# Mean squares of seven norms: partial sums on VectorE in place of products on TensorE

## The reference

```
def rms_norm(x, gain):
    x32 = x.astype(jnp.float32)
    y = x32 * lax.rsqrt(jnp.mean(x32 * x32, axis=-1, keepdims=True) + RMS_EPS)
    return (y * gain.astype(jnp.float32)).astype(x.dtype)
```

## Time and profile before

| what | value |
|---|---|
| median of 3 runs | 3530.77 us |
| profiled execution, its own time | 3534.64 us |
| its span, first to last instruction | 3532.8 us |
| TensorE matmuls busy | 3387.8 us (96%) |
| VectorE busy | 1567.7 us (44%) |
| ScalarE busy | 1187.9 us (34%) |
| GpSimd busy | 1297.5 us (37%) |
| mean granted TensorE clock | 0.983 of full speed |

### The profile page before, as it was taken

How to read it: one execution, slowest core, us unless ns; L and a number is a source line. 1 busy time by engine, 2 the same in 40 slices (tenths; PEclk the granted TensorE clock), 3 DMA queues, 4 the chain that set the end, 5 groups by cost and what they waited for, 6 DMA issues and landing times.

```text
span 3532.8 us, 41630 instructions
## 1 busy us (share of the span) xinstructions
PE 3387.8 (96%) x15852; PEld 2725.5 (77%) x15852; DVE 1567.7 (44%) x2863; ACT 1187.9 (34%) x1638; POOL 1297.5 (37%) x562
## 2 busy tenths in 40 slices
PE   7979999999999999999999999887999999999998
PEld 4667776887888888888888887575788868878886
DVE  5816115996454431165666662417211124642112
ACT  4425223323333333232222222334322234433221
POOL 3320233443333334444444443234344433434442
PEclk9989999999999999999999999999999999999999
DMA  2230222343555456576666663121233322123332
GB/s 106 75 108 25 78 95 74 107 147 111 187 180 193 165 202 200 161 203 188 185 186 190 190 186 117 60 92 34 90 96 94 92 87 72 42 66 95 96 96 78
DMA packets 424645, 428.08 MB, mean 121 GB/s; under 512 B 146720, under 2 KB 343968, under 8 KB 422704
## 3 DMA queue, kind: packets, MB, share of 16 engines
q1 hardware_dynamic: 424496, 426.00, 38.4%
HBM read 354.63 MB, written 69.21 MB: 120 GB/s over the span
## 4 chain that ended last, share of the span: by engine, by line
PE 69%; issue 13%; DVE 11%; POOL 5%; ACT 1%; DMA 1%; SPq 1%; POOLq 0%; DVEq 0%; PEldq 0%; ACTq 0%
PE pb L632 20%; PE pb L633 20%; PE pb L634 20%; POOL s_over L563 5%; PE pb L894 3%; PE pb L649 1%; PE pb L818 1%; DVE s_sq L1539 1%; DVE s_arena L1760 1%; DVE s_arena L1754 1%; DVE s_hS L1553 1%; DMA s_ring<-w 1%; PE pb L803 1%; SPq L443 1%; DVE s_arena L1719 1%
## 5 line engine op out<-in xcount | busy, mean ns | idle before, releaser
L563 POOL TENSOR_TENSOR s_over<-s_ring,s_rhigh 128x1024 fp32r<-128x1024 f32 x518 | 1252.5, 2419 | 2166.3 <-ACT s_rhigh L1168 2166.0
L1168 ACT ACTIVATE s_rhigh<-s_ring 128x1024 fp32r<-128x1024 f32 x518 | 548.7, 1060 | 1504.5 <-DMA s_ring<-w 677.9
L632 PE MATMUL pb<-s_over,s_rhigh 128*128 128x512 f32 x2112 | 835.8, 396 | 0.0
L634 PE MATMUL pb<-s_over,s_over 128*128 128x512 f32 x2112 | 833.7, 395 | 0.0
L633 PE MATMUL pb<-s_over,s_rhigh 128*128 128x512 f32 x2112 | 833.7, 395 | 0.0
L632 PE MATMUL pb<-s_hS,s_rhigh 128*128 128x512 f32 (+1 forms) x1888 | 763.2, 404 | 44.3 <-DVE s_hS L1553 39.8
L634 PE MATMUL pb<-s_hS,s_over 128*128 128x512 f32 (+1 forms) x1896 | 737.3, 389 | 0.0
L633 PE MATMUL pb<-s_hS,s_rhigh 128*128 128x512 f32 (+1 forms) x1888 | 734.9, 389 | 0.0
L633 PEld LDWEIGHTS pb<-s_over,s_rhigh 128*128 128x128 f32 x2112 | 397.2, 188 | 95.6 <-issue 1.2
L632 PEld LDWEIGHTS pb<-s_over,s_rhigh 128*128 128x128 f32 x2112 | 397.2, 188 | 95.5 <-issue 1.2
L634 PEld LDWEIGHTS pb<-s_over,s_over 128*128 128x128 f32 x2112 | 397.2, 188 | 94.5
(11 more groups left out here) (244 smaller groups left out, 2727.1 us busy)
## 6 DMA issues: line engine op xcount, KB each, us to landing
s_ring<-w SPq DMA_DIRECT2D x272, 512.0 KB, 3.5
s_ring<-eu SPq DMA_DIRECT2D x128, 512.0 KB, 4.0
s_ring<-ev SPq DMA_DIRECT2D x128, 512.0 KB, 4.2
acts<-s_arena SPq DMA_DIRECT2D x128, 256.0 KB, 4.0
gates<-s_arena SPq DMA_DIRECT2D x8, 4096.0 KB, 13.8
s_arena<-acts SPq DMA_DIRECT2D x128, 256.0 KB, 4.4
s_arena<-gates SPq DMA_DIRECT2D x128, 256.0 KB, 4.5
s_xT<-xT SPq DMA_DIRECT2D x1, 2048.0 KB, 8.3
```

What stands on the lines that cost most here:

```text
L563: gp.tensor_tensor(rlow[:, s, :, :], ring[:, s, :, :], rhigh[:, s, :, :].bitcast(F32), ALU.subtract).then_inc(S("w_split"), 1)
L632: mm(dst, a_high, b_high, start=start, stop=False)
L634: return mm(dst, a_low, b_high, start=False, stop=stop)
L1168: sc.activation(rhigh[:, s, :, :], ring[:, s, :, :], ACT.Copy).then_inc(S("w_high"), 1)
```

## The change

Norm 0 stays as it was. For norms 1 to 7 the square of chunk 0 is written into a running sum, `sq_sum` (the second half of `rstd`), the squares of chunks 1 to 6 are added to it on VectorE, one between two of its additions to x, and TensorE multiplies the sum and the square of chunk 7: two products for eight. ScalarE's squares move from behind the last tile into the loop over the output tiles, behind the `parts` of each turn. The semaphore `sq_added` is new; some semaphores elsewhere were merged under one name (`pick_step`, `decay_step`, `lz_a`, `lam_a`, `gate_sum`, `gkw_split`) with the counts adapted, the same waits at the same places.

```diff
+        sq_sum = rstd[:, 1, :]
...
+                pe.wait_ge(S("sq_added"), 6 * k)
+                mm(pb[:, MS_BANK[k], :], mat(M_D), sq_sum, start=True, stop=False)
+                pe.wait_ge(S("sq_done"), 8 * k + 8)
+                mm(pb[:, MS_BANK[k], :], mat(M_D), sq[:, 1, :], start=False, stop=True).then_inc(S("sq_used"), 1)
...
-                if o >= 2:
-                    mean_square(4, o - 2)
...
+            def square(k, c, x_before):
+                sc.wait_ge(S("x_upd"), x_before - 7 + c)
+                if c >= 3:
+                    sc.wait_ge(S("sq_added"), 6 * (k - 1) + c - 2)
+                sc.activation(sq_sum if c == 0 else sq[:, c % 2, :], xT[:, c, :], ACT.Square)\
+                    .then_inc(S("sq_done"), 1)
             for o in range(DC):
                 parts(T_OUT + o + 3)
-            norm(1, X_MIX)
+                square(1, o, X_MIX)
+            mean_root(1)
+            highs(1)
...
                 sc.activation(esig[:, o % 2, :], pb[:, 4 + o % 4, :], ACT.Sigmoid).then_inc(S("e_sig"), 1)
+                if o >= 1:
+                    square(3, o - 1, X_PLE)
+            square(3, 7, X_PLE)
...
+            def sum_square(k, c):
+                ve.wait_ge(S("sq_done"), 8 * k + c + 1)
+                if c >= 2:
+                    ve.wait_ge(S("sq_added"), 6 * (k - 1) + c - 1)
+                ve.tensor_tensor(sq_sum, sq_sum, sq[:, c % 2, :], ALU.add).then_inc(S("sq_added"), 1)
             for o in range(DC):
+                if o >= 2:
+                    sum_square(1, o - 1)
                 ve.wait_ge(S("tile_done"), T_OUT + o + 1)
                 add_x(o, o % 4)
```

More of the change, by code:

```diff
@@ L677, in _ @@
             pe.wait_ge(S("consts"), 32)
-            norm(0)
+            norm_first()
             for i in range(22):
@@ L1008, in ffn @@
                         linear(t0, 0, h=hF, hwait=H_NORM[k])
-                        mean_square(k, 7)
+                        norm(k)
                     elif kind == "u":
@@ L1168, in part, with mean_root, highs @@
                 sc.activation(rhigh[:, s, :, :], ring[:, s, :, :], ACT.Copy).then_inc(S("w_high"), 1)
-            def norm(k, x_before):
-                for c in range(DC):
[L1172 to L1189, removed]
+            def square(k, c, x_before):
[4 more added lines that the diff above has]
+                    .then_inc(S("sq_done"), 1)
+            def mean_root(k):
+                sc.wait_ge(S("sq_used"), 8 + k)
+                sc.activation(std[:, 0, :], pb[:, MS_BANK[k], :], ACT.Sqrt, bias=eps).then_inc(S("std_done"), 1)
+            def highs(k):
+                for c in range(DC):
+                    high(H_NORM[k] + c, hS[:, 0, c, :], sq[:, c % 2, :])
+            sc.wait_ge(S("x_in"), 16)
+            sc.wait_ge(S("consts"), 32)
+            for c in range(DC):
+                if c >= 2:
+                    sc.wait_ge(S("sq_used"), c - 1)
+                sc.activation(sq[:, c % 2, :], xT[:, c, :], ACT.Square).then_inc(S("sq_done"), 1)
+            sc.wait_ge(S("sq_used"), 8)
+            sc.activation(std[:, 0, :], pb[:, MS_BANK[0], :], ACT.Sqrt, bias=eps).then_inc(S("std_done"), 1)
+            parts(2)
+            highs(0)
             for i in range(21):
@@ L1346, in _ @@
                 parts(T_V + r + 3)
+                if r >= 120:
+                    square(2, r - 120, X_PEER)
             def norm_plain(k, x0, t0):
@@ L1354, in norm_plain, with hidden @@
                         .then_inc(S("h_high"), 1)
[L1355 to L1360, removed]
+                    square(k, c, x0)
+                mean_root(k)
+            def hidden(t0, e0, k_next, x_next):
                 for i, (kind, j) in enumerate(ffn_tiles()):
@@ L1364, in hidden @@
                     if kind == "v":
+                        if j >= 24:
+                            square(k_next, j - 24, x_next)
                         continue
@@ L1373, in hidden @@
                         act_high(e, j // 8 % 2, k)
-            norm(2, X_PEER)
+            mean_root(2)
+            highs(2)
             for o in range(DC):
@@ L1381, in _ @@
                 sc.activation(esig[:, o % 2, :], pb[:, 4 + o % 4, :], ACT.Sigmoid).then_inc(S("e_sig"), 1)
-            norm(3, X_PLE)
+                if o >= 1:
+                    square(3, o - 1, X_PLE)
+            square(3, 7, X_PLE)
+            mean_root(3)
+            parts(T_AB + 2)
+            highs(3)
             for i in range(8):
@@ L1520, in _ @@
                 high_piece(i)
-            ffn(6, 1, T_F1, X_GLA)
-            norm(7, X_F1)
+            ffn(6, 1, T_F1, X_GLA, X_F1)
+            mean_root(7)
         @block.vector
```

94 lines of the change are left out of this document (49 added, 45 removed).

## The result

| | before | after |
|---|---|---|
| median of the runs | 3533.89 us (4 runs, 3525.6 to 3538.92) | 3501.92 us (4 runs, 3498.23 to 3503.4) |
| ratio | | 0.9911, 95% interval 0.9893 to 0.9929 |
| span of the profiled execution | 3532.8 | 3501.6 |

The changed kernel is 32.0 us faster by the medians, 31.2 by the spans. The forecast was 32.7 and a span of 3500.1. Two launches of the variants further down, 3912.95 us in run 11 and 6778.9 us in run 12, were far slower than all others, and the medians there are taken without them.

What follows compares the result with a forecast made beforehand. TensorE, with a matmul in flight for 96% of the span, was taken to bound the kernel. Terms 14.5 + 4.4 + 3.0 + 10.8 = 32.7 us off the median 3530.77 gave 3498.1; range 3485 to 3512.

Steps and rivals of the forecast that it cites:

- Norms 1, 5, 7: Squares and products leave the path behind the last addition; square root 4.84 us earlier at norm 1, 4.85 at norm 7.
- Norm 2: Square root 4.85 us earlier, but pT's transfer now late, TensorE idles 3.2; gain 4.4, bounds 3.1 and 4.85.
- the cover: At norm 2, 0.9 us left between TensorE reaching the normed x's last chunk and its low part arriving.
- an even chance: Odds given that the clock falls in norm 2's new idle stretch, losing 1.7 us of work, 0.8 behind the cover.
- Norm 3: Root 4.4 us earlier, less 1.4 for square and sum delaying PLE's second half: gain 3.0, bounds 1.2 and 4.7.
- Norms 4 and 6: Six products fewer each between tiles, 0.90 us of TensorE's time apiece: 5.4 each, 10.8 together.
- The added sums: 42 VectorE sums cost nothing outside PLE, with three tiles of cover; in PLE 1.4 us per addition.
- Table loads: Alternating Sigmoid and Square in PLE brings no load; if the skill's rule applied, 2.6 us more, time 3501.
- Median: Forecast time for the changed kernel's median: 3530.77 - 32.7 = 3498.1 us.
- hidden anyway: Rival: norms 4 and 6's products were mostly hidden, the 10.8 us worth nothing, time 3509; chance 0.10.
- The new idling costs the clock more: Rival: clock falls at norms 2 and 3 last into the next tiles, time 3505; chance 0.11.
- The chain turns round: Rival: VectorE's in-order waits let all 42 sums delay TensorE, 1.4 us each, time 3554, slower; chance 0.03.

Runs made afterwards that it cites:

- run 11: run 4's kernel with all eight squares of norms 1 to 7 summed on VectorE, one product per norm; 3507.33 us.
- run 12: changed kernel with VectorE's work per sum doubled in PLE (norm 3) alone; 3501.29 us.
- run 1: changed kernel with sum and two products only in norms 1, 2, 5 and 7, eight products in 3, 4 and 6; 3511.13 us.
- run 5: the changed kernel repeated, in the second group of runs; 3502.46 us.
- run 7: run 4's kernel with pT in its own SBUF place, loaded at the start of the expert layer; 3501.87 us.
- run 3: changed kernel, but norm 3 keeps its eight products and PLE has no squares and sums in its loop; 3503.74 us.
- run 2: changed kernel with sum and two products only in norms 4 and 6, the others as before; 3520.14 us.
- run 4: changed kernel with PLE's square of chunk o-1 ahead of the sigmoid of tile o on ScalarE; 3502.07 us.
- run 6: changed kernel with one more VectorE operation ahead of each of the 36 sums outside PLE; 3505.63 us.
- run 9: run 4's kernel with VectorE's sum in PLE behind the addition, not ahead of the multiplication; 3497.9 us.
- run 10: run 8's kernel with VectorE's sum in PLE behind the addition; 3497.75 us.
- run 8: run 7's kernel with all eight squares summed and one product in norms 4 and 6; 3498.05 us.

## Why the prediction was right, step by step

- **Norms 1, 5, 7**: 4.8, 4.9, 4.9 for 4.84, 4.85, 4.85. Right in size and cause; run 1 shows it without the other norms.
- **Norm 2**: 4.9 in the profiled execution for 4.4. The wait for pT came as forecast (3.04 for 3.2) and the cover held. But "an even chance" for the fall of the clock was too low: of the nine traces with a wait for pT eight show it, and none of the five without. That the profiled execution is the ninth is luck, which hid part of norm 3's miss in the sum. The fall takes 0 to 2.2 of the root to half: run 5 has 36.33 where run 7 without it has 36.32, runs 3 and 1 have 36.92 and 37.21 where run 2 has 35.00. So the term lies between 2.7 and 4.9 from one execution to the next, wider at the low end than my 3.1.
- **Norm 3**: the one term that was mis-sized, 1.5 for 3.0. The delay at the half was right (the wait grew by 1.30, forecast 1.4, and 3.6 was what I said to look for). The estimate left out what a longer wait does to the clock: more work at the lower level behind the half (0.9), and the second product at 1.64 ahead of the root (0.6). 3.0 - 0.9 - 0.6 = 1.5. The bounds had it (1.2 to 4.7), though the low one for another reason, both products at the lower clock, and nothing for the work behind the half. The 1.5 also hangs on the execution of before, whose clock fell at the half: run 2 has the same PLE and norm 3 with the clock held, and takes 73.85 from root to root, less than the 74.11 of the changed kernel. The medians of runs 3 and 4 (1.7 apart) are too scattered to add to this.
- **Norms 4 and 6**: 5.3 and 5.5 for 5.4 each. Between tiles nothing hid a product, and run 2 alone brings 10.4 of 10.8.
- **The added sums**: nothing outside PLE, as forecast; runs 5 and 6 put a further 36 at 0.09 each, part of which is the clock's and all of which is within the scatter. Inside PLE the step's price was right (1.30 for 1.4) and its reason half right: as run 4 shows, a sum inside the split lasts until 0.5 behind its end, and as run 9 shows, it doesn't have to stand there.
- **Table loads**: PLE has one, ahead of its first sigmoid (at 2224.33 before, at 2219.56 after), although squares now stand between the sigmoids. The Trainium skill's rule in "ScalarE: Activation LUTs", section "Table sets: the hidden batching unit", which I had weighed for Square and Sigmoid, does not bite for this pair.
- **Median**: 3501.92 for 3498.1. Of the 3.8, 3.1 is the kernel before, whose median went from 3530.77 (3 runs) to 3533.89 (4 runs) with one run more; 3533.89 - 32.7 = 3501.2. That so little is left is partly luck: in the profiled execution norm 2 gave 0.5 more than forecast where norm 3 gave 1.5 less, and with the clock down behind pT, as in eight traces of nine, norm 2 would have given up to 2.2 less.

On the rivals: "hidden anyway" was tested and fell. "The new idling costs the clock more" was half of it: one fall grew at the half, the one at norm 2 is usual but wasn't in this trace. "The chain turns round" doesn't happen here, and run 6 shows where it would begin.

## What to carry to other kernels

Price a removed instruction by where it stands: on TensorE's stream at its issue time (0.90 us for an fp32 product of 128x512), in an exposed chain at the whole hand-over (six for 4.85, 0.8 each), and keep the one product there that fills a wait. When an accumulation moves to another engine, put it behind the operation that releases someone, not in front of it (run 10 against run 8: 2.5 us for an order). When the new order makes TensorE wait longer somewhere, add the price of the clock to each wait that has grown.

## What the runs showed that I had not expected

- At the same place of the same code the granted clock falls in one launch and holds in another. At 302 to 314 us, which none of the variants touches, it was 1.00 in before, run 1 and run 7, 0.57 in after and 0.51 in run 4. Norm 1's last addition ended at 541.4 in run 3 and at 547.7 in run 4, more than a norm's gain apart. Before spreads over 13 us, so differences of 2 or 3 us between variants were read from distances within the trace.
- At the half a wait of 2.2 us left the clock at 1.00 in four traces and at 0.83 in two; a wait of 3.5 or more had it down in all eight (0.66 or 0.83).
- VectorE's multiplication of a PSUM and an SBUF tile isn't held up by GpSimd's split (0.69 at 2232.11, inside the split of run 9), while the sum of two SBUF tiles is (2.44 in run 4). The Trainium skill, "SBUF — State Buffer", section "Who interferes with whom", makes that difference between one and two SBUF inputs; these two rows agree with it. In these rows an operation with two SBUF inputs ends some 0.54 behind the split's recorded end, or after its own 0.69, whichever is later: 2234.77 for 2234.23 in run 4, 2237.78 for 2237.23 in the changed kernel; so the addition at 2232.84 in run 9, with a split that ends at 2232.91, loses nothing. The split waits for VectorE too: in run 6 the one at 3125.94, begun while VectorE's maximum of 3125.78 (0.68) ran, took 2.77, where those shown for the other kernels took 2.35 to 2.37.
